# A transformer kernel on one core: eight small copies go to SP's queue, and the conv norm moves ahead of the output projection

## The reference, cut to what matters

```python
def hybrid_mixer(h, cos, sin, w_in, q_a_norm, w_uq, kv_a_norm, w_ukv, conv_w, attn_out_norm, conv_out_norm, w_o):
    proj = h @ w_in
    c_q, c_kv, k_pe, gate_b, gate_c, val = jnp.split(proj, offs, axis=-1)      # 384, 256, 32, 512, 512, 512 columns
    q = (rms_norm(c_q, q_a_norm) @ w_uq).reshape(B, S, 8, 96)                  # 64 plain + 32 rotary columns a head
    q_nope, q_pe = jnp.split(q, [64], axis=-1)
    kv = (rms_norm(c_kv, kv_a_norm) @ w_ukv).reshape(B, S, 8, 128)
    k_nope, v = jnp.split(kv, [64], axis=-1)
    q_pe, k_pe = apply_rope(q_pe, cos, sin), apply_rope(k_pe[:, :, None, :], cos, sin)
    k_full = jnp.concatenate([k_nope, jnp.broadcast_to(k_pe, (B, S, 8, 32))], axis=-1)
    attn = causal_attention(concatenate([q_nope, q_pe]), k_full, v).reshape(B, S, 512)
    conv = gate_b * causal_short_conv(gate_c * val, conv_w)                    # 3 taps
    merged = jnp.concatenate([rms_norm(attn, attn_out_norm), rms_norm(conv, conv_out_norm)], axis=-1)
    return merged @ w_o
```

## Time and profile before

| what | value |
| --- | --- |
| median of 3 runs | 3434.24 us (3428.83 to 3437.14) |
| the profiled execution, its own time | 3434.24 us |
| its span, from the first to the last instruction | 3432.5 us (1.7 us lie around it) |
| mean granted TensorE clock | 0.973 of full speed |
| PE busy | 3265.4 us, 95% of the span |
| DVE busy | 1817.9 us, 53% |
| ACT busy | 1181.4 us, 34% |
| POOL busy | 989.2 us, 29% |

### The profile page before, as it was taken

One profiled execution on the slowest core, in us unless ns is written; L12 is line 12 of the kernel. 1 busy time (PEld: TensorE's weight loads), 2 busy tenths in 40 slices (PEclk: granted clock), 3 DMA queues, 4 the chain that ended last, 5 costly groups with the idle time before them and its releaser, 6 DMA issues.

```text
span 3432.5 us, 40313 instructions
## 1 busy us (share of the span) xinstructions
PE 3265.4 (95%) x14533; PEld 2601.4 (76%) x14533; DVE 1817.9 (53%) x2457; ACT 1181.4 (34%) x1780; POOL 989.2 (29%) x691
## 2 busy tenths in 40 slices
PE   6999999999999999999999998999999999899998
PEld 4888866678887888766788876767777777678887
DVE  5554465655545433565645434446776674375443
ACT  3222245432223222344422223454333231343332
POOL 2994000069804700000098500001894000021000
PEclk9999999999999999999999998999999998899999
DMA  6664342266634633321376433113664344143332
GB/s 210 205 205 136 94 120 55 62 185 203 183 98 149 183 95 96 89 70 49 93 208 201 149 96 98 50 37 101 200 203 134 91 118 81 49 128 99 98 92 86
DMA packets 576304, 420.32 MB, mean 122 GB/s; under 512 B 28715, under 2 KB 535962, under 8 KB 575046
## 3 DMA queue, kind: packets, MB, share of 16 engines
q1 hardware_dynamic: 536562, 285.04, 28.2%
q0 software_dynamic: 34464, 123.75, 12.4%
q10 hardware_dynamic: 5172, 10.17, 1.0%
HBM read 413.10 MB, written 8.68 MB: 123 GB/s over the span
## 4 chain that ended last, share of the span: by engine, by line
PE 83%; DVE 11%; ACT 3%; issue 2%; DMA 1%; ACTq 0%; SPq 0%; DVEq 0%
PE bank L325 24%; PE bank L327 24%; PE bank L326 24%; PE bank L1326 2%; PE bank L1354 2%; DVE w_lo L306 2%; DVE tmp L450 2%; DVE h_lo L460 1%; PE bank L1340 1%; PE bank L431 1%; DVE folded L510 1%; PE bank L2481 1%; PE bank L409 1%; PE bank L357 1%; DMA raw<-in_w_in 1%
## 5 line engine op out<-in xcount | busy, mean ns | idle before, releaser
L325 PE MATMUL bank<-h_hi,w_hi 128*128 128x512 f32 x2656 | 1059.9, 399 | 53.7 <-DVE h_lo L460 21.3
L327 PE MATMUL bank<-h_hi,w_lo 128*128 128x512 f32 x2656 | 1046.1, 394 | 0.0
L326 PE MATMUL bank<-h_lo,w_hi 128*128 128x512 f32 x2656 | 1045.6, 394 | 0.0
L306 DVE TENSOR_TENSOR w_lo<-raw,w_hi 128x1024 fp32r<-128x1024 f32 x438 | 657.5, 1501 | 570.6 <-ACT w_hi L289 568.7
L289 ACT ACTIVATE w_hi<-raw 128x1024 fp32r<-128x1024 f32 x438 | 462.0, 1055 | 653.0 <-PE bank L327 653.0
L325 PEld LDWEIGHTS bank<-h_hi,w_hi 128*128 128x128 f32 x2656 | 504.5, 190 | 190.9 <-DVE h_lo L460 37.2
L327 PEld LDWEIGHTS bank<-h_hi,w_lo 128*128 128x128 f32 x2656 | 504.3, 190 | 108.7
L326 PEld LDWEIGHTS bank<-h_lo,w_hi 128*128 128x128 f32 x2656 | 505.1, 190 | 103.3 <-issue 0.5
L693 POOL TENSOR_TENSOR mod_acc<-mod_acc,mod_w 128x1024 f32<-128x1024 f32 x168 | 434.1, 2584 | 14.0
L325 PE MATMUL bank<-hid_hi,w_hi 128*128 128x512 f32 x1056 | 412.8, 391 | 6.0 <-DVE w_lo L306 5.5
L327 PE MATMUL bank<-hid_hi,w_lo 128*128 128x512 f32 x1056 | 411.7, 390 | 0.0
(11 more groups left out here) (356 smaller groups left out, 3337.7 us busy)
## 6 DMA issues: line engine op xcount, KB each, us to landing
raw<-in_ffn_w_gu SPq DMA_DIRECT2D x176, 512.0 KB, 4.5
mod_w<-in_w_ada POOLq DMA_DIRECT2D x128, 512.0 KB, 4.0
mod_w<-in_mod_w POOLq DMA_DIRECT2D x96, 512.0 KB, 4.2
raw<-in_ffn_w_in SPq DMA_DIRECT2D x88, 512.0 KB, 3.7
raw<-in_ffn_w_down SPq DMA_DIRECT2D x64, 512.0 KB, 4.0
raw<-in_w_in SPq DMA_DIRECT2D x34, 512.0 KB, 3.7
raw<-in_ffn_w_out SPq DMA_DIRECT2D x32, 512.0 KB, 4.0
raw<-in_ffn_w_down SPq DMA_DIRECT2D x32, 384.0 KB, 3.3
```

Source lines behind the costliest of these rows:

```text
L306: loop(nc.vector.tensor_tensor(w_lo[:, u % 2, :], raw[:, u % 2, :], w_hi[:, u % 2, :].bitcast(F32), ALU.subtract), "split_lo", times)
L325: nc.tensor.matmul(dst, a_hi, b_hi, start=start, stop=False)
L326: nc.tensor.matmul(dst, a_hi, b_lo, start=False, stop=False)
L327: return nc.tensor.matmul(dst, a_lo, b_hi, start=False, stop=stop)
```

## The change

Four edits, all in the mixer. (1) The wait for `kpe_ready` and the eight copies into `k_full` leave POOL and stand on SP, between the loads of units 10 and 11. (2) `conv_sum` comes ahead of all matmuls of the output projection, `conv_spread` after its second step, and the convolution steps of its first two column blocks alternate between the blocks. (3) On ACT `conv_root` stands ahead of the last split, on DVE `conv_invert` and the last split stand ahead of the second `a_lo`. (4) The sum and the spread of the attention norm come one step later within the last unit of `w_in`.

```diff
--- before.py
+++ after.py
@@ -1455,6 +1455,12 @@
             wq = d["w_uq"][l].rearrange("(kt p) n -> p kt n", p=P)
             for a, b in UQ_HEADS:
                 load(sp, wq[:, :, a * HD:b * HD], 3 * (b - a) * HD, pattern="p (kt n) -> p kt n", n=(b - a) * HD)
+                if a == 0:
+
+                    wait(sp, "kpe_ready", key)
+                    src = work[0:ROPE, 0, :]
+                    for h in range(HEADS):
+                        done(sp.dma_start(k_full[NOPE:HD, h, :], src), "kpe_spread", key, 16)
             wkv = d["w_ukv"][l].rearrange("(kt p) (h part c) -> part kt p h c", p=P, part=2, c=NOPE)
             for part in range(2):
 
@@ -1465,13 +1471,6 @@
             for n in range(FRONT, len(mla_units())):
                 unit(n)
             sp_out(sp, d["w_o"][l], KT)
-
-        def pool_mla(pool, key):
-
-            wait(pool, "kpe_ready", key)
-            src = work[0:ROPE, 0, :]
-            for h in range(HEADS):
-                done(pool.dma_start(k_full[NOPE:HD, h, :], src), "kpe_spread", key, 16)
 
         def mla_jobs(key):
             jobs = []
@@ -1630,9 +1629,9 @@
                     c = slice(kt * P, (kt + 1) * P)
                     ins = mm3(psum[1][:, :], w_hi[:, s, c], w_lo[:, s, c], h_hi[:, kt, :], h_lo[:, kt, :], kt == 0,
                               kt == KT - 1)
-                    if h == HEADS - 1 and kt == 3:
+                    if h == HEADS - 1 and kt == 4:
                         norm_sum(pe, (key, "attn"), 3)
-                    if h == HEADS - 1 and kt == 5:
+                    if h == HEADS - 1 and kt == 6:
                         norm_spread(pe, (key, "attn"), 3)
                 unit_end(ins)
             after_hidden(pe)
@@ -1642,7 +1641,9 @@
 
             def begin(pe):
 
-                for mm, kts in ((0, range(4)), (1, range(4)), (0, range(4, 8)), (1, range(4, 8))):
+                conv_sum(pe, key, 4)
+                for mm, kts in ((0, range(4)), (1, range(4)), (0, (4,)), (1, (4,)), (0, (5,)), (1, (5,)), (0, (6,)),
+                                (1, (6,)), (0, (7,)), (1, (7,))):
                     s = (u0 + mm) % 2
                     pe.wait_ge(sg.sem("split_lo"), u0 + mm + 1)
                     for kt in kts:
@@ -1650,8 +1651,6 @@
                         c = slice(kt * P, (kt + 1) * P)
                         ins = mm3(psum[5 + mm][:, :], w_hi[:, s, c], w_lo[:, s, c], b_hi(kt), b_lo(kt), kt == 0, kt == KT - 1)
                         if mm == 0 and kt == 1:
-                            conv_sum(pe, key, 4)
-                        if mm == 1 and kt == 0:
                             conv_spread(pe, key, 4)
                         if kt == KT - 1:
                             done(ins, "unit_used")
@@ -1767,8 +1766,8 @@
             round_attn(0)
             conv_square(act, key, 3)
             round_attn(1)
+            conv_root(act, key, 4)
             split_hi(act)
-            conv_root(act, key, 4)
             round_attn(2)
             round_attn(3)
             norm_round(act, (key, "conv"), 4, None, lambda m: c_hi[:, m, :])
@@ -1885,12 +1884,12 @@
             conv_take(dve, key, FRONT + HEADS - 1, v0 + HEADS)
             scale(1)
             low(0)
+            conv_invert(dve, key)
+            split_lo(dve)
             low(1)
             scale(2)
-            split_lo(dve)
             scale(3)
             low(2)
-            conv_invert(dve, key)
             low(3)
             wait(dve, "norm_lo", ((key, "attn"), 3))
             norm_scale_split(dve, (key, "conv"), 4, 4, lambda m: conv[:, m, :], lambda m: col(("conv_out_norm", l), m), None,
@@ -2914,8 +2913,6 @@
             mod_begin(pool)
             for key in PHASES:
                 mod_sums(pool, key)
-                if key[0] == "m":
-                    pool_mla(pool, key)
                 if key[0] == "o":
                     pool_odd(pool, key)
```

## The result

| kernel | median us | runs |
| --- | --- | --- |
| before, beside the changed kernel | 3435.08 | 5 |
| changed | 3452.73 (3449.10 to 3457.91) | 5 |
| ratio | 1.0054, 95% interval 1.0039 to 1.0069 | |

The changed kernel is slower by 17.7 us. The forecast was 12.4 us slower. Two more comparisons gave 1.0049 (1.0035 to 1.0062) and 1.0042 (1.0030 to 1.0054), and medians 12.5 to 19.3 us apart. The profiled execution took 3450.88 us (span 3449.1, mean granted clock 0.970).

A forecast was written before the change was run, and what follows sets the result against it. PE, busy 95% of the span, was taken to bound the kernel. Per mixer, 4.0 us stop, 1.5 clock and 0.7 end make 6.2, for two 12.4: 3434.2 + 12.4 = 3446.6, stated as 3446.5 us, range 3438 to 3453.

The forecast's parts named there:

- The wait itself: On SP ahead of unit 11: `kpe_ready` comes at 490.05, so load 11, before at 479.95, goes out ten microseconds later.
- Issues: On SP between the wait and load 11: eight copy issues take 3.80 us, with ends of 2.3 and 4.9 us.
- Landing and ACT's chain: Front: load 11 lands 3.4 us after issue; ACT's split-to-square 0.95, square 0.62 and query 0.59 us follow.
- Clock: Behind PE's front stop: half clock for about 3.4 us loses 1.5 us per mixer, ends 0 and 1.6.
- End: Mixer's end: block 0 ends last but one, so the third block starts 0.7 us later; ends -0.7 and +1.5.
- The forecast of the parts: Mixer's end: convolution tiles ready 2 us earlier, but alternating steps end block 0 later, at 641.9 instead of 641.1.
- the longer stop with a longer half clock: Copies in flight delay the load, 5.0 us stop; second half-clock stretch at the end, +1.5; 3450.4 us, 11%.
- The rival without any delay: Front: SP's issues cost nothing, PE stops 0.3 us, clock doesn't fall; 3436.2 us, chance 5%.
- the short-issue one: Front: copies issue like the cheapest small loads, 2.5 us stop, no clock fall; 3440.6 us, chance 20%.

The follow-up runs named there:

- the four-copies kernel: Against the kernel before: copies moved from POOL to SP, the wait and four copies ahead of unit 11's load, four copies behind unit 12's; measured 1.0011.

## Why the prediction came out as it did

The mechanism was right, and two sizes at the front were too small. I had 4.0 us of stop, 1.5 of clock and 0.7 of end in each mixer, 6.2 together. The runs showed 5.4 of stop, 2.6 of clock and about nothing at the end, 8.0 together. So the forecast failed on two terms of its sum, the eight issues on SP and the half clock behind the stop; that the end was set too high hid a part of it, which is luck.

- **The wait itself: right.** It decides nothing but that the slack is gone (0.16 us of stop with the wait alone).
- **Issues: mis-sized.** I took 3.80 us for eight, from stores of 64 KB; measured 5.05, or 0.63 each. I had the other end, 4.94, and set it aside as a start after a long rest. From this step come 1.3 us a mixer. The reason did not hold: with four copies ahead and four behind, the four after SP's wait took 2.52 us and the four straight behind the loads 2.43, so a rest is worth 0.1 us there and not 1.1.
- **Landing and ACT's chain: right.** 495.65 to 499.20 is 3.55 (predicted 3.4), and 499.20 to 501.31 is 2.1 (predicted 2.16). The Trainium skill (DMA: Bandwidth & Descriptors, Issuing engines are not separate DMA queues) calls the time of an issue usually small beside the transfer. In the changed kernel's trace the issue of one copy took 0.63 us against 2.0 us from issue to landing: less than the transfer, but not small, and eight in a row add up to 5.05 us.
- **Clock: mis-sized.** I took one half-clock stretch of 3.4 us, 1.5 us of loss. Behind stops of 5.3 and 5.5 us it lasted 6.8, twice that, and the swap at its start took 1.91 us instead of 0.97. The front is 8.0 us in the traces, the stop 5.4, so 2.6 are the clock's, as the kernels with PE kept busy also say. Behind the 2.86 us stop of the four-copies kernel it was one stretch of 3.4. So the two errors go together at this place: of twelve fronts with a stop of 5.2 to 5.6 us eleven had 6.8 us of half clock and one 13.7, and the four with 2.7 to 2.9 us had 3.4. Why the longer stop has the longer fall is not shown.
- **End: its term was 0.7, and is about nothing.** With and without edit 1 the timed runs put edits 2 to 4 at zero, give or take 3 us for both mixers. The forecast of the parts held: the convolution tiles are ready earlier, and the alternation gives it back at the third block. What I did not see is how large both sides are: the new place of the sums and the spread (with DVE's order in either of two forms) is worth 11 us, and the alternation takes about 8 of them, 3 to 13 by the two intervals.
- **Edit 4** was not run by itself. Its cost is inside that zero.

With the two sizes put right, the steps give 2 x (5.3 + 2.6) = 15.8 us at the front. The three comparisons gave 17.7, 19.3 and 12.5, a mean of 16.5. Of the rivals, the longer stop with a longer half clock, 3450.4 us, comes nearest in number, but not by its reasons: the stop grew by the issues and not by copies in flight, which shows only with one large DMA, and the second stretch of half clock came at the front and not at the end. The rival without any delay is out, and so is the short-issue one.

**What stays open.** Edit 1 alone was timed at 10.6 and 12.5 us (11.0 and 13.1 by the ratios), less than the 16 of its traces. The profile of before is not to blame at the front: eleven of twelve fronts without a delay lie within 0.1 us of its own. One place further on gives some of it back. PE of the kernel before stops 2.31 us up to 2643.22, and then runs at half clock for 3.4:

```profile
2643.22 0.50 PE L325 MATMUL bank<-hid_hi,w_hi 128*128 128x512 f32 x1 [2.31 <-DVE w_lo L306]
```

```profile
2643.60:2647.00 3.40, 3.40 (x10) 2.63 (x9) 1.85 (x5) 1.37 (x3) 0.00 (x0) 0.50 0.51 154
```

Edit 1 alone (second profile) stops 1.65 us there and keeps its full clock:

```profile
2662.92 0.50 PE L325 MATMUL bank<-hid_hi,w_hi 128*128 128x512 f32 x1 [1.65 <-DVE w_lo L306]
```

All eleven profiles with copies on SP regain 2.2 or 2.3 us at this place; of the six others besides before, five regain nothing and one 1.6. That is 2.3 of the 3 to 5 us that are missing. Why they do, and where the remainder goes, was not separated. And the share of ACT's order (root ahead of the split; `w_lo` waits 0.77 us for it on DVE) was not tried apart.

## What to carry to other kernels

Before you put DMA issues ahead of a load on the same queue, count the issues, take the longest length that the trace shows for such a one, and see whether the load still has that much slack: a wait that is just hidden leaves none. Behind the load the same issues are free. When two accumulations share their last steps, end the one that the next stage waits for first; alternating them cost about 8 us here. And size a clock fall with a stop of the same length at a like place: at the front here, a longer stop had the longer fall, while at the end the same code had falls of 3.4 to 10.2 us from one profile to the next.

## What the runs showed of the hardware

- An SP issue of a copy within SBUF of 32 rows by 512 took 0.60 to 0.63 us, in every kernel and place (5.02 to 5.06 for eight, 2.41 to 2.52 for four). The two loads of units 11 and 12 behind eight of them took 1.14 together; behind one DMA of 512 KB, 2.57.
- A 432 KB load issued behind one 512 KB copy reached ACT after 5.25 us; behind eight copies of 64 KB issued over 5 us it took 3.5.
- Behind the front's stops of 2.7 to 2.9 us the clock was at half for 3.4 us, behind stops of 5.2 to 5.6 for 6.8 in eleven of twelve cases and for 13.7 in one. 20 unused matmuls in such a stop kept the clock full.
- How long such stretches are in unchanged code moves from profile to profile: at the mixer's end 3.4 us in before and 10.2 us in three kernels with the same end. The kernel before ranged from 3430.74 to 3443.84 us in one comparison, 0.4%.
